# Attention by pairs of heads on the column halves of TensorE, with the softmax denominators summed on GpSimd

## The reference

```python
def block_attention(q, k, v, sink=None):
    ...
    scale = hd ** -0.5

    def one(qblk):
        s = jnp.einsum('bqkgd,bskd->bkgqs', qblk, k).astype(F32) * scale
        if sink is not None:
            sk = jnp.broadcast_to(sink.astype(F32).reshape(KV, G)[None, :, :, None, None], s.shape[:-1] + (1,))
            p = jax.nn.softmax(jnp.concatenate([s, sk], axis=-1), axis=-1)[..., :-1]
        else:
            p = jax.nn.softmax(s, axis=-1)
        return jnp.einsum('bkgqs,bskd->bqkgd', p.astype(v.dtype), v)
```

## Time and profile before

| what | value |
|---|---|
| time of three runs, us | 2260.01, 2261.18, 2265.01 (median 2261.18) |
| the profiled execution's own time, us | 2266.69 |
| its span in the profile, us | 2264.9 |
| mean granted clock of TensorE | 0.933 of 2.4 GHz |
| busy, share of the span | PE 88%, PEld 58%, DVE 41%, ACT 35%, POOL 8% |
| chain that ended last, by engine | PE 68%, issue 10%, DVE 5%, POOL 4% |

### The profile page before, as it was taken

One profiled execution on the slowest core, in us unless ns is written; L12 is line 12 of the kernel. 1 busy time (PEld: TensorE's weight loads), 2 busy tenths in 40 slices (PEclk: granted clock), 3 DMA queues, 4 the chain that ended last, 5 costly groups with the idle time before them and its releaser, 6 DMA issues.

```text
span 2264.9 us, 30150 instructions
## 1 busy us (share of the span) xinstructions
PE 1988.2 (88%) x12212; PEld 1312.2 (58%) x12212; DVE 924.5 (41%) x1875; ACT 786.0 (35%) x1663; POOL 184.6 (8%) x259
## 2 busy tenths in 40 slices
PE   3978999997999989897979999878978977878898
PEld 1644555543565544774647765458567567476386
DVE  2665444312333364434643321462452462552442
ACT  2552444510222224313535551234333333432431
POOL 0000000000000000000000000025024033042000
PEclk8997999998999999998979999888988978988999
DMA  8020000021000224332020002210110100101232
GB/s 300 29 77 1 0 1 1 1 113 58 1 1 1 75 81 166 127 136 100 19 68 1 1 11 106 62 29 3 26 29 2 33 32 11 54 3 67 71 102 94
DMA packets 61292, 118.38 MB, mean 52 GB/s; under 512 B 5048, under 2 KB 27724, under 8 KB 61025
## 3 DMA queue, kind: packets, MB, share of 16 engines
q1 hardware_dynamic: 40033, 57.53, 7.7%
q0 software_dynamic: 8640, 33.75, 4.3%
q10 hardware_dynamic: 12480, 25.17, 3.1%
HBM read 96.47 MB, written 19.96 MB: 51 GB/s over the span
## 4 chain that ended last, share of the span: by engine, by line
PE 68%; issue 10%; DVE 5%; POOL 4%; PEld 4%; DMA 3%; ACT 3%; DVEq 1%; PEldq 1%; POOLq 0%; ACTq 0%; SPq 0%
PE ps L532 8%; PE ps L835 8%; PE ps L946 6%; PE ps L1003 6%; PEld ps L1761 4%; PE ps L1330 3%; PE ps L1170 3%; PE ps L1355 3%; PE ps L1171 3%; PE ps L1172 3%; PE ps L790 2%; PE ps L817 2%; PE ps L816 2%; PE ps L804 2%; DMA work<-in_w_mod 1%
## 5 line engine op out<-in xcount | busy, mean ns | idle before, releaser
L835 PE MATMUL ps<-work 128*128 128x512 f32 (+3 forms) x512 | 232.0, 536 | 0.0
L859 DVE TENSOR_REDUCE work<-ps 128x1 f32<-128x512 f32 (+2 forms) x272 | 145.2, 561 | 199.6 <-PE ps L790 198.9
L909 ACT ACTIVATE work<-ps 128x512 f32<-128x512 f32 (+3 forms) x256 | 132.1, 517 | 193.8 <-PE ps L817 141.7
L1761 PE MATMUL ps<-hT,wring 128*128 128x512 f32 (+1 forms) x576 | 190.1, 492 | 8.0 <-SPq L2134 5.5
L532 PE MATMUL ps<-wring,hT 128*128 128x512 f32 (+2 forms) x576 | 192.9, 493 | 0.0
L816 PE MATMUL ps<-qA,kA 128*128 128x512 f32 (+3 forms) x256 | 171.7, 671 | 2.1 <-ACT work L900 1.7
L1761 PEld LDWEIGHTS ps<-hT,wring 128*128 128x128 f32 x576 | 95.9, 193 | 103.6 <-issue 99.5
L532 PEld LDWEIGHTS ps<-wring,hT 128*128 128x128 f32 x576 | 109.1, 192 | 78.5 <-issue 70.3
L946 PE MATMUL ps<-hT,wring 128*128 128x512 f32 (+1 forms) x384 | 128.6, 497 | 4.0 <-DVEq L184 4.0
L1003 PE MATMUL ps<-wring,hT 128*128 128x512 f32 x288 | 125.8, 599 | 5.2 <-SPq L1549 3.4
L790 PE MATMUL ps<-kA,qA 128*128 128x128 f32 (+3 forms) x336 | 101.0, 351 | 27.0 <-DVE work L859 14.7
(11 more groups left out here) (291 smaller groups left out, 3499.6 us busy)
## 6 DMA issues: line engine op xcount, KB each, us to landing
work<-in_w_mod ACTq DMA_DIRECT2D x10, 2048.0 KB, 13.5
work<-in_x_sample SPq DMA_DIRECT2D x16, 512.0 KB, 6.5
wring<-in_w_in_even POOLq DMA_DIRECT2D x4, 2048.0 KB, 9.2
out_y_sample<-work SPq DMA_DIRECT2D x16, 512.0 KB, 3.0
work<-out_y_sample SPq DMA_DIRECT2D x16, 512.0 KB, 5.0
wring<-in_w_in_odd POOLq DMA_DIRECT2D x3, 2048.0 KB, 8.7
wring<-in_w_in_odd POOLq DMA_DIRECT2D x12, 512.0 KB, 6.4
yA_gated<-work SPq DMA_DIRECT2D x8, 576.0 KB, 3.3
```

Of the source, the lines that this page charges most:

```text
L835: pe.matmul(ps[:, 5 + c_, (qa - q0) * P:(qb - q0) * P], vaug[:, h // 4, kt, :], pT[i % 3][:, 0:(qb - qa) * P], start=(first and l == 0), s ...
L859: v.tensor_reduce(dst, src, AX.X, ALU.max).then_inc(sm("mx_used"), 1)
L909: act.activation(pT[i % 3][:, 0:n], ps[:, ST_BANKS[i % len(ST_BANKS)], 0:n], ACT.Exp, scale=0.125).then_inc(sm("p_done"), 1)
L1761: mm = pe.matmul(ps[:, PROJ_BANK[n], 0:m], w[:, k, b * P:(b + 1) * P], hT[:, k, o:o + m], start=(k == 0), stop=(k == KD - 1))
```

## The change

Heads go in pairs. The two heads of a pair share their stationary values `vv`, now 64 columns without the ones, and their value products go to output partitions 0 to 63 and 64 to 127, the two column halves of the array. Four `pT` buffers (in the tile `gg`) hold two items of two heads; each head has one score bank (2 and 3), and values come one item behind the scores.

The denominators no longer come out of the value product. For a chunk's first item DVE copies `pT` to `s_sum` (layer 1: adds the sinks' exponentials to one row of it), and GpSimd adds every later item, `att_pool`. Three products against ones (`den`, bank 4) sum over the keys, and ACT (`ri`) and DVE (`out`) work on 128 partitions for both heads, at later steps than before.

The negated maxima are transposed by one matmul and copied to `a_nmT` (ACT). A DMA from SP's queue (`att_sp`) lays them out as a row. The maxima of the next pair's two heads are spread over the current pair's items, at three places of each item: after the first score, after the second, and after the values. The first pair's two heads have theirs ahead of the first score. The context chunk comes first now. The staging address of one weight load (`gateA1`) moves, and a memset of the ones in `vaug` (L621) goes.

```diff
-        vaug = qr.take(2 * 10 * P).rearrange("p (g t n) -> p g t n", g=2, n=P)
+        vv = qr.take(2 * 10 * HD).rearrange("p (g t n) -> p g t n", g=2, n=HD)
...
-        qB = [take_rounded(ar2, f"qB{i}", T) for i in range(2)]
-        qB_plain = [Region(qB_at + i * T).take(T) for i in range(2)]
+        qB = [take_rounded(ar2, f"qB{i}", T) for i in range(4)]
+        qB_plain = [Region(qB_at + i * T).take(T) for i in range(4)]
         ES = slice(96, 97)
-        pT = [ar2.take(512) for _ in range(3)]
+        pT = [gg[:, i // 2, 512 * (i % 2):512 * (i % 2) + 512] for i in range(4)]
+        s_sum = [[ar2.take(512) for _ in range(2)] for _ in range(2)]
...
-            v.memset(vaug[:, :, :, HD:P], 1.0)
...
-        CHUNKS = [(0, 4), (4, 8), (8, 9)]
+        CHUNKS = [(8, 9), (0, 4), (4, 8)]
...
-        AHEAD = 2
-        ST_BANKS = (2, 3, 4)
+        NP = [len(x) for x in PRODUCTS]
+        ST_BANKS = (2, 3)
+        DEN_BANK = 4
+        ROW_BANK = 1
...
+            n = NP[l]
+            half = n // 2
+            def ahead(pair, p):
+                a, b = 2 * pair, 2 * pair + 1
+                if p < half - 1:
+                    for m in range(MU[l] * p // (half - 1), MU[l] * (p + 1) // (half - 1)):
+                        yield "max", a, m
+                elif p == half - 1:
+                    yield "row", a, 0
+                elif p < n - 3:
+                    w = n - 3 - half
+                    for m in range(MU[l] * (p - half) // w, MU[l] * (p - half + 1) // w):
+                        yield "max", b, m
+                elif p == n - 3:
+                    yield "row", b, 0
+                elif p == n - 1 and l == 1:
+                    yield "sink", a, 0
+                    yield "sink", b, 0
+            for p in range(n):
+                yield from ahead(0, p)
+            todo = []
+            for i in range(4 * n + 1):
+                beside = list(ahead(i // n + 1, i % n)) if i // n < 3 else []
+                third = -(-len(beside) // 3)
+                if i < 4 * n:
                     yield "scores", i, 0
-                    if h < 7:
-                        if p < spread:
-                            for m in range(MU[l] * p // spread, MU[l] * (p + 1) // spread):
-                                yield "max", h + 1, m
-                        elif spread < p <= spread + 3:
-                            yield "row", h + 1, p - spread - 1
-                if i >= AHEAD:
-                    yield "values", i - AHEAD, 0
-                    if items[i - AHEAD][6]:
-                        yield "out", items[i - AHEAD][0], items[i - AHEAD][4]
+                    yield from beside[:third]
+                    yield "scores", i, 1
+                    yield from beside[third:2 * third]
+                if i:
+                    v = i - 1
+                    yield "values", v, 0
+                yield from beside[2 * third:]
+                if i:
+                    if PRODUCTS[l][v % n][5]:
+                        todo.append((v + 2, "den", 3 * (v // n) + PRODUCTS[l][v % n][3]))
+                        todo.append((v + 3, "ri", 3 * (v // n) + PRODUCTS[l][v % n][3]))
+                        todo.append((v + 4, "out", 3 * (v // n) + PRODUCTS[l][v % n][3]))
+                    while todo and (todo[0][0] <= v or i == 4 * n):
+                        _, what, x = min(todo)
+                        todo.remove(min(todo))
+                        yield what, x, 0
+                    todo.sort()
...
+        def att_sp(sp, l):
+            base = items_so_far(l)
+            for h in range(8):
+                sp.wait_ge(sm("row_out"), 8 * l + h + 1)
+                if h >= 4:
+                    sp.wait_ge(sm("s_ps"), 2 * (base + NP[l] * (h // 2 - 1)))
+                sp.dma_start(qB[h % 4][HD:HD + 1, :].bitcast(F32), a_nmT[h % 2][0:NT, :].bitcast(F32)).then_inc(sm(f"rows_in{h % 2}"), 16)
+        def att_pool(pool, l):
+            base = items_so_far(l)
+            for i in range(4 * NP[l]):
+                pair, kt, qa, qb, N, (q0, q1), first, last = item(l, i)
+                if first:
+                    continue
+                pool.wait_ge(sm("sum_first"), 12 * l + N + 1)
+                pool.wait_ge(sm("p_done"), 2 * (base + i) + 2)
+                pool.drain()
+                for j in range(2):
+                    to = s_sum[N % 2][j][:, (qa - q0) * P:(qb - q0) * P]
+                    mm = pool.tensor_tensor(to, pT[2 * (i % 2) + j][:, 0:(qb - qa) * P], to, ALU.add)
+                mm.then_inc(sm("sum_added"), 1)
...
-                    h, r = x, y
+                    h = x
                     pe.wait_ge(sm("nm_done"), 8 * l + h + 1)
-                    if r == 2:
-                        pe.wait_ge(sm("row_out"), 3 * (8 * l + h) + 1)
-                    for t in range(*ROW_TILES[r]):
-                        mm = pe.matmul(ps[HD:HD + 1, (MU[l] + r) % 2, (t - ROW_TILES[r][0]) * P:(t - ROW_TILES[r][0] + 1) * P],
-                                       a_nm[h % 2][:, t:t + 1], ident, start=True, stop=True)
-                    mm.then_inc(sm("row_ps"), 1)
+                    pe.transpose(ps[0:NT, ROW_BANK, 0:P], a_nm[h % 2], ident).then_inc(sm("row_ps"), 1)
...
-                    i = x
-                    h, kt, qa, qb, c_, first, last = PRODUCTS[l][i]
-                    nb = len(ST_BANKS)
-                    if first and c_ == 0:
-                        pe.wait_ge(sm("row_out"), 3 * (8 * l + h) + 3)
-                    if i >= nb:
-                        pe.wait_ge(sm("p_done"), base + i - nb + 1)
-                    s_ = ps[:, ST_BANKS[i % nb], 0:(qb - qa) * P]
+                    i, j = x, y
+                    pair, kt, qa, qb, N, _, first, last = item(l, i)
+                    h, n = 2 * pair + j, 2 * i + j
+                    if i % NP[l] == 0:
+                        pe.wait_ge(sm(f"rows_in{h % 2}"), 16 * (4 * l + h // 2 + 1))
+                    if n >= 2:
+                        pe.wait_ge(sm("p_done"), 2 * base + n - 1)
+                    s_ = ps[:, ST_BANKS[j], 0:(qb - qa) * P]
...
-                    h, kt, qa, qb, c_, first, last = PRODUCTS[l][i]
-                    q0, q1 = CHUNKS[c_]
-                    if first and h:
-                        pe.wait_ge(sm("y_done"), 3 * (8 * l + h - 1) + c_ + 1)
-                    pe.wait_ge(sm("p_done"), base + i + 1)
-                    if first and l == 1:
-                        pe.matmul(ps[:, 5 + c_, 0:(q1 - q0) * P], sumrow[ES, :], qB_plain[h % 2][ES, q0 * P:q1 * P],
-                                  start=True, stop=False, skip_group_check=True)
-                    pe.matmul(ps[:, 5 + c_, (qa - q0) * P:(qb - q0) * P], vaug[:, h // 4, kt, :],
-                              pT[i % 3][:, 0:(qb - qa) * P], start=(first and l == 0), stop=last,
-                              skip_group_check=True).then_inc(sm("pv_ps"), 1)
+                    pair, kt, qa, qb, N, (q0, q1), first, last = item(l, i)
+                    if first and pair:
+                        pe.wait_ge(sm("y_done"), 12 * l + N - 2)
+                    pe.wait_ge(sm("p_done"), 2 * (base + i) + 2)
+                    for j, rows in enumerate((LOW, HIGH)):
+                        mm = pe.matmul(ps[rows, 5 + N % 3, (qa - q0) * P:(qb - q0) * P], vv[:, pair // 2, kt, :],
+                                       pT[2 * (i % 2) + j][:, 0:(qb - qa) * P], start=first, stop=last, skip_group_check=True)
+                    mm.then_inc(sm("pv_ps"), 1)
+                elif what == "den":
+                    N = x
+                    q0, q1 = CHUNKS[N % 3]
+                    sums_wait(pe, l, last_item(l, N))
+                    if N:
+                        pe.wait_ge(sm("ri_done"), 12 * l + N)
+                    for j, rows in enumerate((LOW, HIGH)):
+                        mm = pe.matmul(ps[rows, DEN_BANK, 0:(q1 - q0) * P], ones[:, 0:HD], s_sum[N % 2][j][:, 0:(q1 - q0) * P], start=True, stop=True)
+                    mm.then_inc(sm("den_ps"), 1)
...
+                elif what == "values":
+                    i = x
+                    pair, kt, qa, qb, N, (q0, q1), first, last = item(l, i)
+                    if not first:
+                        continue
+                    v.wait_ge(sm("p_done"), 2 * (base + i) + 2)
+                    if N >= 2:
+                        v.wait_ge(sm("den_ps"), 12 * l + N - 1)
+                    m = (q1 - q0) * P
+                    for j in range(2):
+                        mm = v.tensor_copy(s_sum[N % 2][j][:, 0:m], pT[2 * (i % 2) + j][:, 0:m])
+                    if l == 1:
+                        v.wait_ge(sm("es_done"), 2 * pair + 2)
+                        v.drain()
+                        for j in range(2):
+                            mm = v.tensor_tensor(s_sum[N % 2][j][ES, 0:m], s_sum[N % 2][j][ES, 0:m],
+                                                 qB_plain[(2 * pair + j) % 4][ES, q0 * P:q1 * P], ALU.add)
```

(23 more changed lines are left out.)

136 lines of the change are left out of this document (58 added, 78 removed).

## The result

The changed kernel takes 2234.77 us (median of 4 runs, 2234.36 to 2237.61) against 2260.69 (4 runs on the same chip, 2260.01 to 2265.01): ratio 0.9884, 95% interval 0.9867 to 0.9901. It is faster by 26 us where 63 were forecast; the time lies inside the range, 37 us above the predicted one. The profiled execution took 2234.82 us, its span is 2232.9.

The account below looks back on a forecast made before the run. TensorE's matmul stream, with a lead-in, was taken to bound both attention stages. Layer 0 -33.0, layer 1 -29.5 and the memset -1.1 sum to -63.6 us: 2203 profiled, 2198 median, range 2160 to 2242.

Parts of the forecast that it names:

- GpSimd: the term that failed: GpSimd's attention additions: 1.10 us each, 2.35 per item, hidden in layer 0's pairs 1 to 3, bounding pair 4 at 42.6.
- if PE idles between items in pairs 1 to 3: Sign that the forecast is wrong: TensorE standing idle between items in the first three pairs.
- rival (b): GpSimd bounds the attention throughout, at 1.5 to 1.81 us per addition: 2212 to 2240 us; chance 0.15.
- DVE's reductions: In layer 0's pairs, four items with bunched maxima, where DVE holds TensorE some 0.4 us each: 1.6 us per pair.
- rival (c): New waits for exponentials with one score bank per head, all earlier waits kept, 0.2 us more per item: 2232; chance 0.15.
- Layer 1's last pair: Pair 4 of layer 1, without maxima and rows: 24 us, plus 3.5 us of tail.
- rival (a): The two column halves run one after the other, 0.85 us more per value pair: about 2300, slower; chance 0.06.
- The layout change: TensorE's switch from full array to halves and back, each item: 0.30 us, 5.7 per layer-0 pair, 3.9 per layer-1 pair.
- rival (d): Layout changes are hidden, -33 us, and there is none of the bunching: 2160; chance 0.14.
- The lead-in: Both heads of pair 1 need their maxima before any score: 43.8 us in layer 0, 23.8 in layer 1.
- The wait ahead of the row: TensorE waits for DVE's negated maxima before the transpose: 0.8 us, twice per pair.
- ACT waiting for POOL only in pair 4: Sign expected in the profile after: ACT's exponentials wait for GpSimd in the fourth pair alone.

Follow-up runs that it names:

- e2: Changed kernel with GpSimd's additions cut to 8 columns (DVE's first copy also adds 1.0), work left out: 2206.0 us.
- e4: Changed kernel with DVE's layer-0 maxima reduced over only 16 columns and a smaller exponential scale, work left out: 2207.7 us.
- e6: Changed kernel with a third pair of sum buffers, all work kept: 2228.2 us, ratio 0.9845.
- e12: Changed kernel with each chunk's den, ri and out steps one item earlier: 2228.0 us, ratio 0.985.
- e8: Changed kernel with four banks instead of two for the first pair's maxima in the lead-in: 2220.2 us, ratio 0.9817.
- e10: Changed kernel with third sum buffers, four lead-in banks, and DVE making the second head's additions in each layer's last pair: 2204.3 us, ratio 0.9744.
- e5: Changed kernel with layer 0's row step one item behind the last maxima, which are packed into one item fewer: 2238.4 us, ratio 0.9893.
- e13: e10 with the den, ri and out steps one item earlier, as in e12: 2196.1 us, ratio 0.9708.
- e11: e10 with DVE making the second head's additions in all four pairs of layer 0: 2213.4 us, ratio 0.9786.

## Why the prediction was right in sign and wrong in size

The profiled execution was forecast at 2203 and took 2234.8, 31.6 more. By the windows: layer 0's lead-in -4.6, its pairs 1 to 3 +14.0, pair 4 with its tail +10.4; layer 1's lead-in -6.6, pairs 1 to 3 +8.8, pair 4 with its tail +7.8; the rest of the program +1.8 (+0.7 against the -1.1 of the memset).

**GpSimd: the term that failed.** "I take 1.10: an item costs POOL 2 x 1.10 + 0.15 = 2.35 ... So POOL is hidden in pairs 1 to 3 (37.6 of 55.5 us) and bounds pair 4 ... = 42.6". Measured: 1.30 per addition, 2.67 per item, and 10 us of stops per pair where 5.0 were counted in pair 4 and none mattered in pairs 1 to 3. By these a layer-0 pair comes to 52.8 us, 10 above the 42.6. Mechanism and place were right for pair 4, which e2 brings to 46.9 us; the size was wrong. "Hidden" was wrong too: with 52.8 us of 55.5 used, it holds only if nothing else is late. This is the sign "if PE idles between items in pairs 1 to 3", and it came: PE is busy 56.1 of pair 2's 59.9 us. e2 returns 9.6 of pair 4's 10.4 us, 8.2 of the 14.0 in pairs 1 to 3, and 6.6 in layer 1. The rival (b), POOL as the bound throughout, had the price wrong (1.5 us) and the outcome nearly right. Its upper end was added up wrongly: at 1.81 us an item is 3.77, and a pair 60.3 + 5 = 65.3, not 62.9; the forecast doesn't rest on it.
The Trainium skill, "GPSIMD Engine Reference", section Performance versus the Vector engine, gives about 2.6 cycles for each element of a two-input addition, at the engine's 1.2 GHz. An estimate from that figure is 2.17 ns a column and 1.11 us for 512, to which the dispatch is added. The trace agrees (2.20 ns a column, 1.30 us in all). The forecast had not weighed it.

**DVE's reductions: a term that was too small.** The forecast had 1.6 us per pair, "four items with their units bunched ... where DVE ... holds PE some 0.4 us", and 1.0 more for all other waits. e4, with short reductions and GpSimd's additions whole, brings layer 0's pairs 1 to 3 to 54.0 to 54.7 us, 17.5 us shorter together and under the forecast's 55.5. So GpSimd and DVE's reductions together hold these pairs up. The 14.0 us can't be shared out between them: each experiment alone gives back 8.2 (e2) or 17.5 (e4, with some of the clock), and no run has both.

**New waits: unforeseen in this form.** The forecast looked for waits of ACT between items, the rival (c). What came are handovers between chunks: the sum buffer, held by a late denominator product, and in layer 1 the one denominator bank (6.5 us of PE's waits). e6 and e12 take some 8 us each off the two stages. With (b) and (c) both partly true, 2234.8 lies where the forecast had put each alone (2212 to 2240 and 2232). That is luck and confirms neither price.

**Layer 1's last pair: wrong.** "35.0 - 7.4 - 2.6 - 1.0 = 24". The pair took 35.3 with its tail against 27.5. Maxima and rows were taken off as if PE were busy to the end; PE is busy 27.5 of 35.3 us there. Neither short additions (33.4) nor one full product besides (32.3) brings it near; earlier steps and the mends do in part (30.3). The 2.8 us that are left are not settled; PE is busy 25.9 of these 30.3 us, at a clock of 1.00 throughout. The changed kernel's pair has in it the wait of 2.74 us for the denominator bank, 3.4 us at 0.50 behind it, and in its tail 1.7 us for GpSimd's last additions. Also, 171.7 / 8 x 2 = 42.9 leaves out that the last head has no maxima and rows, which the sum for layer 0 did put in; with the same 7.4 / 2 + 2.8 it is 44.6, and the forecast of pairs 1 to 3 would be 1.6 us higher each.

**The clock: not counted.** Pair 1 of layer 0 is 2.6 us longer than pair 2, and 3.4 in e2, where GpSimd isn't in the way. In the lead-in PE waits for DVE ahead of many of its products, and the granted clock is 0.50 (1.2 GHz) there and for another 12.5 us, to about 219.2; in the kernel before it was 1.00 in layer 0 from the first scores on the earlier trace rows. Three windows of the changed kernel at the start of pair 1:

```profile
209.20:213.30 4.10, 4.02 (x12) 2.66 (x12) 1.58 (x3) 1.21 (x3) 0.00 (x0) 0.50 0.00 0
213.30:217.00 3.70, 3.70 (x14) 2.34 (x13) 1.94 (x5) 1.20 (x3) 0.00 (x0) 0.50 0.00 0
217.00:219.50 2.50, 2.50 (x8) 0.84 (x8) 1.48 (x4) 0.26 (x1) 0.27 (x1) 0.56 0.00 0
```

Two other things differ between the pairs: PE waits 1.40 us for head 1's row at the start of pair 1, and the stop for the sum buffer stands only in pair 2. The nearest price of the clock is in e8 and e10, which have the same lead-in of 27.4 us. In e8 the clock is 1.00 from 7 us after the first score, in e10 from 11 us; e8's fifth item starts 13.3 us into the pair and e10's 15.2. So 4 us longer at 0.50 went with 1.9 us, though e10 has two more edits. In layer 1 the clock is 0.50 for the first 12.9 us of pair 1 and for 3.4 us in each of the others (0.84 and 0.95 over the windows above; 0.98 before), and the forecast had no term for that.

**Right.** Halves overlap (rival (a) had 0.06). The layout change costs 0.27 us in layer 0 and 0.17 in layer 1 where 0.30 was taken, so rival (d) falls. PE's count of pairs 2 and 3 is near: 56.1 to 56.4 us without the additions against 55.5, with DVE's share still in them. The lead-in was overestimated (39.2 and 17.2 against 43.8 and 23.8): the first score belongs to head 0, whose row has long arrived, and only the second score, 2.6 us later, waits for head 1's DMA. The wait ahead of the row is 1.25 us in steady pairs where 0.8 was taken, and by e5 moving it is worth nothing while it packs the maxima closer.
The sign "ACT waiting for POOL only in pair 4" nearly held: 17.4 us there, 1.9 in pair 3, none before. It was a bad sign: in pairs 2 and 3 POOL's lateness reaches ACT through DVE's first copies (2.9 us at the start of each), which wait for a denominator product.

**Still open** is how the 58.5 us of e13's pairs 2 and 3 divide: PE is busy 54.6 of them, POOL needs some 51 with its stops, and DVE's reductions set PE's short waits between. No run took out one of them alone with the mends in place. How much of each gain in layer 1 is a wait and how much the clock behind it is open too.

## What to carry to other kernels

Work that moves to an idle engine has to be priced in the shape and with the operands that it will have there, and its sum compared with the pace of the stream it joins: with nearly all of the cover used, each of its stops is paid by all. Where a chunk ends, write down for each buffer which late step frees it and who stands behind the one that waits; such edits (a third buffer, the steps one item earlier), two more banks in the lead-in and DVE's help where it is idle gave as much again as the change itself, and more (39 us against 26). Finely spread work is part of the gain: with the same instructions at one place of each item nothing was left of the gain. Read the granted clock of both windows before a difference between them is put down to an edit.

## What the runs showed of the hardware

**A DVE operation on two SBUF operands stretches GpSimd's addition beside it.** In e10's pair 4 of layer 0 DVE (L959) and GpSimd (L845) each add one head, at the same time:

```profile
390.62 0.69 DVE L959 TENSOR_TENSOR work<-gg,work 128x512 f32<-128x512 f32 x1 [1.26 <-ACT gg L1008]
390.75 1.71 POOL L845 TENSOR_TENSOR work<-gg,work 128x512 f32<-128x512 f32 x1 [0.45 <-ACT gg L1008]
```

GpSimd takes 1.71 us instead of the 1.25 to 1.27 of L834 in the changed kernel. DVE's maxima, which read PSUM, do no such thing: with them cut short in e4 an addition still takes 1287 ns (mean) against 1301. The stretch works both ways: in e11 DVE's additions take 953 ns in the mean, 692 in e10.

```profile
L959 DVE TENSOR_TENSOR work<-gg,work 128x512 f32<-128x512 f32 x64 | 61.0, 953 | 32.4 <-ACT gg L1008 28.7
```

```profile
L959 DVE TENSOR_TENSOR work<-gg,work 128x512 f32<-128x512 f32 x16 | 11.1, 692 | 23.1 <-ACT gg L1008 23.1
```

The query copy, whose type changes from f32 to fp32r, takes 1111 ns beside the additions in the changed kernel and 744 in e2. The Trainium skill, "GPSIMD Engine Reference", section Key points, names two kinds of DVE instruction, with two SBUF inputs and in 2-port modes, as the ones that contend with GpSimd. The additions are of the first kind, and their rows agree: 0.44 us more on GpSimd, 0.26 on DVE. The query copy is stretched by 0.37 us; that it runs in a 2-port mode no run here shows.
